# An attention cycle's roundings, rescalings and read-outs placed anew over its slots; FOX's scaling with two factors

## The reference, cut to what matters

```
p_cmp = masked_softmax(q . k_cmp * scale, blk_end <= t)          # 31 compressed keys
o_cmp = p_cmp @ v_cmp
o_slc, o_win = masked_softmax(rope(q) . rope(k) * scale, causal) @ v   # two branches
nsa   = (g0 * o_cmp + g1 * o_slc + g2 * o_win) * silu(z_a)
fox   = (masked_softmax(q . k * scale + F_q - F_k, causal) @ v) * silu(z_b)
x     = x + (sigmoid(r_a) * (nsa @ w_nsa) + sigmoid(r_b) * (fox @ w_fox)) @ w_out
```

## Time and profile before

| what | value |
| --- | --- |
| median of 3 runs | 1475.65 us |
| the profiled execution: time | 1475.33 us |
| the profiled execution: span in the profile | 1473.6 us |
| TensorE, VectorE, ScalarE, GpSimd busy | 98%, 70%, 62%, 34% of the span |
| granted TensorE clock, mean | 0.999 of full |

### The profile page before, as it was taken

How to read it: one execution, slowest core, us unless ns; L and a number is a source line. 1 busy time by engine, 2 the same in 40 slices (tenths; PEclk the granted TensorE clock), 3 DMA queues, 4 the chain that set the end, 5 groups by cost and what they waited for, 6 DMA issues and landing times.

```text
span 1473.6 us, 22913 instructions
## 1 busy us (share of the span) xinstructions
PE 1440.1 (98%) x7490; PEld 1223.7 (83%) x7490; DVE 1025.3 (70%) x2431; ACT 910.2 (62%) x1912; POOL 499.2 (34%) x578
## 2 busy tenths in 40 slices
PE   9999999999999999999999999999999999999998
PEld 7887888888888788888888888888888887888887
DVE  6847888888888874444576588888888887644444
ACT  6636888778788752223464487788778777422234
POOL 2303664565566420000021145654665564000000
PEclk9999999999999999999999999999999999999999
DMA  8232212212121233333453312212121212433332
GB/s 281 76 98 59 58 44 58 58 44 58 44 58 44 58 117 98 100 100 87 112 181 91 98 48 54 58 43 59 44 58 47 55 45 55 139 92 100 99 100 90
DMA packets 201626, 118.29 MB, mean 80 GB/s; under 512 B 9304, under 2 KB 195888, under 8 KB 201008
## 3 DMA queue, kind: packets, MB, share of 16 engines
q1 hardware_dynamic: 199120, 107.49, 26.7%
q0 software_dynamic: 1728, 8.66, 1.6%
q10 hardware_dynamic: 672, 0.83, 0.2%
HBM read 110.54 MB, written 6.42 MB: 79 GB/s over the span
## 4 chain that ended last, share of the span: by engine, by line
PE 82%; DVE 8%; ACT 5%; issue 3%; POOL 0%; DVEq 0%; ACTq 0%; POOLq 0%
PE acc L1906 52%; PE o_pair L2005 6%; PE turned L1980 6%; PE scores L1963 3%; PE scores L1965 3%; PE turned L2234 2%; ACT q_fox L909 2%; DVE prob L1465 2%; PE scores L2234 1%; DVE q_fox L1377 1%; ACT w_hi L860 1%; DVE pt_lo L1477 1%; PE turned L2158 1%; PE o_pair L2013 1%; DVE qk_raw L1333 1%
## 5 line engine op out<-in xcount | busy, mean ns | idle before, releaser
L1906 PE MATMUL acc<-u_hi,w_hi 128*128 128x512 f32 x968 | 380.4, 393 | 0.0
L1906 PE MATMUL acc<-u_lo,w_hi 128*128 128x512 f32 x968 | 378.9, 391 | 0.0
L1906 PE MATMUL acc<-u_hi,w_lo 128*128 128x512 f32 x968 | 375.8, 391 | 0.0
L1290 DVE TENSOR_TENSOR w_lo<-w_raw,w_hi 128x1024 fp32r<-128x1024 f32 x184 | 228.0, 1239 | 116.6 <-ACT w_hi L860 115.9
L860 ACT ACTIVATE w_hi<-w_raw 128x1024 fp32r<-128x1024 f32 x184 | 193.1, 1050 | 132.4 <-PE acc L1906 79.4
L981 ACT ACTIVATE prob<-prob,row_max 128x256 f32<-128x256 f32 (+3 forms) x308 | 172.7, 561 | 134.0 <-DVE row_max L1465 128.6
L1906 PEld LDWEIGHTS acc<-u_hi,w_lo 128*128 128x128 f32 x968 | 181.8, 188 | 34.8
L1906 PEld LDWEIGHTS acc<-u_hi,w_hi 128*128 128x128 f32 x968 | 181.8, 188 | 34.7 <-issue 0.2
L1906 PEld LDWEIGHTS acc<-u_lo,w_hi 128*128 128x128 f32 x968 | 181.9, 188 | 33.5 <-issue 0.2
L783 POOL TENSOR_SCALAR prob<-prob,row_inv,gates 128x384 f32<-128x384 f32 (+3 forms) x205 | 137.1, 669 | 203.2 <-DVE row_inv L1472 202.4
L1477 DVE TENSOR_TENSOR pt_lo<-turned,pt_hi 128x384 fp32r<-128x384 f32 (+3 forms) x384 | 169.6, 482 | 3.5 <-ACT pt_hi L990 3.5
(11 more groups left out here) (337 smaller groups left out, 2783.3 us busy)
## 6 DMA issues: line engine op xcount, KB each, us to landing
w_raw<-in_w_in_dram SPq DMA_DIRECT2D x140, 512.0 KB, 3.7
w_raw<-in_w_proj_nsa_dram SPq DMA_DIRECT2D x16, 512.0 KB, 3.8
w_raw<-in_w_proj_fox_dram SPq DMA_DIRECT2D x16, 512.0 KB, 3.8
w_raw<-in_w_out_dram SPq DMA_DIRECT2D x16, 512.0 KB, 3.8
x_scratch<-xT POOLq DMA_DIRECT2D x2, 2048.0 KB, 8.2
xT<-x_scratch POOLq DMA_DIRECT2D x2, 2048.0 KB, 8.7
x_nat<-in_x_dram SPq DMA_DIRECT2D x4, 512.0 KB, 6.1
c_w<-in_cmp_w_k_dram SPq DMA_DIRECT2D x4, 512.0 KB, 5.5
```

What stands on the lines that cost most here:

```text
L1290: dve.tensor_tensor(w_lo[:, par, :, 0:width], w_raw[:, par, :, 0:width], w_hi[:, par, :, 0:width], ALU.subtract).then_inc(w_lo_done, 1)
L1906: ins = pe.matmul((bank or acc[par])[0:width, :], own_w, rhs, start=(n == 0), stop=(n == 23))
```

## The change

The number of instructions of TensorE, ScalarE and VectorE stays as it is. What changes is where they stand:

- TensorE: `cmp_turn` from slot 5 to 7, `cmp_values` of head 0 from 11 to 13, and `Plan`'s costs with it: two matmuls each move from slot 7 to slot 5 and one from slot 13 to 11 (in the last cycle likewise).
- ScalarE: `cmp_copy` from slot 7 to 10; the tanh of FOX's z two slots earlier, of NSA's z one slot later.
- VectorE: `split_lo` one slot later, but for the unit whose loop index is 0; `qf_rest` one head at a time, the second two slots later; `kf_rest` of head 0 one or two slots later; FOX's z read one slot earlier; NSA's z read and silu one slot later; the read of FOX's head 1 from slot 7 to 8; `cmp_rest` from slot 8 to 12.
- GpSimd: FOX's probabilities are scaled by the reciprocal and by a column of ones, in the form of instruction that NSA's have with their gate.

```diff
-        for s, cost in ((1, 2.0), (5, 2.0), (11, 1.0), (19, 1.0)):
+        for s, cost in ((1, 2.0), (7, 2.0), (13, 1.0), (19, 1.0)):
...
-                if branch is None:
-                    ins = pool.tensor_scalar(p, p, row_inv[:, ring:ring + 1], None, ALU.mult)
-                else:
-                    gate = gates[:, qt, bass.ds(2 * pair.i + HEADS * branch + h, 1)]
-                    ins = pool.tensor_scalar(p, p, row_inv[:, ring:ring + 1], gate, ALU.mult, ALU.mult)
-                ins.then_inc(s_scaled, 1)
+                gate = ones[:, 0:1] if branch is None else gates[:, qt, bass.ds(2 * pair.i + HEADS * branch + h, 1)]
+                pool.tensor_scalar(p, p, row_inv[:, ring:ring + 1], gate, ALU.mult, ALU.mult).then_inc(s_scaled, 1)
...
-                at(plan.end[z] + 4, lambda: z_tanh_of(fox.r, 1))
+                at(plan.end[z] + 2, lambda: z_tanh_of(fox.r, 1))
                 if not cycle.first:
-                    at(max(0, Plan().end[4] + 1 - CYCLE_STEPS) + 2, lambda: z_tanh_of(nsa.r, 0))
+                    at(max(0, Plan().end[4] + 1 - CYCLE_STEPS) + 3, lambda: z_tanh_of(nsa.r, 0))
...
-                at(7, cmp_copy)
+                at(10, cmp_copy)
...
-            def qf_rest(parts):
+            def qf_rest(parts, heads):
 
                 dve.wait_ge(part_hi_done, parts + 1)
-                for h in range(2):
+                for h in heads:
                     ins = dve.tensor_tensor(q_fox[other(h), h, 0, :], qk_raw[own(h), :], q_fox[own(h), h, 0, :],
                                             ALU.subtract)
-                ins.then_inc(part_lo_done, 1)
+                if 1 in heads:
+                    ins.then_inc(part_lo_done, 1)
...
-                        at(slot + 1, lambda u=u: split_lo(*cycle.unit(u + 1)))
+                        at(slot + (2 if u else 1), lambda u=u: split_lo(*cycle.unit(u + 1)))
...
-                at(plan.end[0] + 3, lambda: qf_rest(parts))
+                at(plan.end[0] + 3, lambda: qf_rest(parts, (0,)))
+                at(plan.end[0] + 5, lambda: qf_rest(parts, (1,)))
...
-                at(key + 3, lambda: kf_rest(parts + 1, (0,), nsa.m))
+                at(key + (4 if cycle.first or cycle.last else 5), lambda: kf_rest(parts + 1, (0,), nsa.m))
...
-                at(plan.end[z] + 2, lambda: z_raw_of(*cycle.unit(z), fox.r, 1))
+                at(plan.end[z] + 1, lambda: z_raw_of(*cycle.unit(z), fox.r, 1))
...
-                    late = max(0, Plan().end[4] + 1 - CYCLE_STEPS)
+                    late = max(0, Plan().end[4] + 1 - CYCLE_STEPS) + 1
...
-                    at(7, lambda: head_output(before, 1))
+                    at(8, lambda: head_output(before, 1))
...
-                at(8, cmp_rest)
+                at(12, cmp_rest)
...
-                for slot, what in ((1, cmp_scores), (5, cmp_turn), (11, lambda: cmp_values(0)),
+                for slot, what in ((1, cmp_scores), (7, cmp_turn), (13, lambda: cmp_values(0)),
```

## The result

The changed kernel takes 1450.93 us (median of 4 runs, 1450.17 to 1451.44); the kernel before, on the same chip, 1475.42 (median of 4). The ratio is 0.9834, 95% interval 0.9817 to 0.9851. Forecast were 1450.7 and a range of 1446 to 1461. The profiled execution took 1450.78, its span is 1449.1 (before 1475.33 and 1473.6).

A forecast was written before the change was run, and what follows sets the result against it. TensorE, busy 98% of the span, bounds the kernel, so only its holes can be won: 12 x 1.45 + 2 x 1.73 + 2 x 2.0 = 24.9 us off, giving 1450.7; range 1446 to 1461.

The forecast's parts named there:

- the mechanism of slot 10: Middle cycles: a transposition waits for VectorE's pt_lo of step 4, late by queues on VectorE and ScalarE; 1.45 us each, 12 times.
- the z slots: New slots for z read-outs: free VectorE early, head 0's y_all 0.6 us sooner; nothing gained on TensorE's path in middle cycles.
- w_lo's move: VectorE's split_lo one slot later: slot 7's maximum is ready by about 228.9, so ScalarE goes on at 229.36 instead of 230.16.
- the last cycles: Last attention cycle of each layer: holes of together 3.22 us close, a new 1.3 opens; net about 2.0, bounds 0.8 and 3.2.
- The order on both engines: VectorE's and ScalarE's queues before slot 10: pt_lo ready at 234.55 and 234.95, covers of 0.6 and 0.5 before TensorE asks.
- The first cycles: First attention cycle of each layer: its whole hole of 1.73 us goes; its slot 5 wait for a maximum stays.
- the holes of 0.55, 0.84 and 1.01: Three of four TensorE holes in each layer's last cycle, the 0.55 for y_all; claimed to close by the same moves.
- kf_lo's new wait: Last cycles: key's remainder of head 0, moved from slot 14 to 15, ends after TensorE comes; new hole of 1.3 us.
- Rival B: Hole closes partly or returns two slots on, VectorE and GpSimd contending in slot 10; 1457 to 1463; 0.25 with upper C.
- Rival C: Edit misses the cause: q_fox on ScalarE starts no earlier, only pc_t's 0.77 is won; 1463; chance within B's 0.25.
- Rival D: Slower: compression chain becomes the bound, its cover falling from 5.3 to 2.5; 1490 if 5 late; chance 0.06 with its like.
- q_fox: FOX's query remainder on VectorE: second head, 0.69 us, leaves slot 8 for slot 10, shortening the queue ahead of pt_lo.

## Why the prediction was right

The total and the mechanism of slot 10 came as forecast. One step was wrong and didn't show in the total, the z slots; two were mis-sized, what w_lo's move is worth and the last cycles.

*What bounds it, and the slot 10 hole.* Right, but for a detail: the view of waits doesn't end with the three rows that the prediction calls all of them. Three more, ahead of the first attention cycle, hold 2.4 us (1.7, 0.5 and 0.2), and 2.3 of it is still there. The hole was all pt_lo, and it closed in every middle cycle: 1.51 saved in each but one, where 1.45 was said. That one, the fourth of layer 0, had been 51.86 before and gave 1.75.

*The order on both engines.* Right to 0.3 us. The prediction let VectorE end pt_lo of step 5 at 234.95, 17.17 into the cycle; it ended at 16.95. The transposition was put at 17.35 and came at 17.34.

*ScalarE.* pt_hi of step 4 was to be ready at 15.6 into the cycle; it starts at 14.97 and the pair ends at 15.84.

*The first cycles.* 1.73 said, 1.63 measured. *The last.* 2.0 said, 1.5 measured. kf_lo's new wait was said as 1.3 and is 1.39. The wrong step is "the holes of 0.55, 0.84 and 1.01 close by the same moves": that of slot 10 stays with 0.77. There w_lo stands ahead of slot 9's remainders and, begun 0.16 behind a scaling on GpSimd, takes 1.68 instead of 1.2. The prediction had weighed this contention only for slot 10 of the middle cycles.

Sum: 2 x 1.63 + 11 x 1.51 + 1.75 + 2 x 1.5 = 24.6 us, against 24.9 forecast.

*The z slots: the step that was wrong, in a sum that is right.* "None of it is on TensorE's path in middle cycles: nothing gained." Taken as an edit to the kernel before that is so (1474.83). In the change it isn't: w_lo's move needs it. With w_lo alone, and with compression and w_lo, y_all of slot 3 ends 6.37 into the cycle, behind the 6.18 at which TensorE asks. It isn't TensorE's gain that makes it late: with the compression alone TensorE gains 1.03 a cycle and y_all stays in time at 5.83, and with w_lo alone TensorE gains nothing and waits. The prediction followed w_lo to slots 7 and 11 and to its own reader, but not in slot 21, ahead of the next cycle's head; and it had y_all 0.6 sooner by the z slots and used that for the last cycles alone. The z slots bring it to 4.74. Without them 9.2 of the 24.5 us are gone. Only because the part was in the change did the total come out: that much was luck.

*w_lo: undersized.* The prediction had it as what makes ScalarE's q_fox start 0.8 earlier. The runs show a second and larger effect, 28.9 us in company against 3.2 alone: it takes w_lo out of slot 10, where q_fox's second head and GpSimd's y_all now stand. Rival B, at 0.25, named the meeting but not what keeps it away. The wait it spoke of, up to 1.3, is 0.98. The 2.00 by which the cycle is longer is more than the 0.4 to 0.8 of B, but it holds w_lo's own 1.23 too, and no run has the one without the other.

*q_fox.* The prediction counted 0.69 off VectorE's queue for it. With y_all's 0.68 put in its place this is nothing, as the 1451.52 without it shows.

*The two factors.* Sum and cost right: 0, shown by 1450.84.

*Rival C* is out: q_fox on ScalarE starts 12.19 into the cycle instead of 13.11. *Rival D* is out for the changed kernel: the compression's remainder ends at 237.76, 2.4 before its use at 240.17, where 2.5 was said. Its mechanism showed in the last cycle with the compression alone and without w_lo (1.0 and 1.3 of waiting).

Without w_lo's move the cycle is 2.00 longer: 0.35 at slot 10, 1.31 at slot 12, and 0.26 right behind that, where the third transposition of the slot waits for the next remainder. Two things stay open. The key's new slot in the middle cycles was never tried by itself. And that it is the w_lo of slot 21 which makes y_all late is read from the traces; no run moved that one alone.

## What to carry to other kernels

Parts of a schedule change don't add. Alone these four parts give -11.5, -3.2, +16.0 and -0.6 us, about +0.8 in sum; together, and with the key's new slot, they give -24.5. So an operation that is moved must be followed in every slot where it now stands, along its engine's queue to each reader, and over the cycle's end: w_lo's move pays in slot 10 and costs in slot 3 of the next cycle. And what runs on the other engine in the same place counts too: two engines with separate queues can still be one queue.

## What the runs showed of the hardware

GpSimd's one-factor scaling of 128x512 takes twice as long as the two-factor one, in one kernel, without the two factors (busy us, mean ns | idle before):
```profile
L783 POOL TENSOR_SCALAR prob<-prob,row_inv,gates 128x512 f32<-128x512 f32 x51 | 39.5, 774 | 63.1 <-DVE row_inv L1474 63.1
L780 POOL TENSOR_SCALAR prob<-prob,row_inv 128x512 f32<-128x512 f32 x25 | 39.2, 1567 | 6.9 <-DVE row_inv L1474 6.9
```
In the changed kernel FOX's 25 take 774 in the mean, as NSA's do. The 2024 of the earlier trace rows held some waiting beside it: of those 25 the median is 1571, the longest 2617. The shorter form was worth nothing in time here. The Trainium skill ("GPSIMD Engine Reference", section 3.1) would have both forms at one price; the measurement decides against it for this pair.

VectorE's operations on two SBUF inputs and GpSimd's exclude each other nearly for their whole length, and the one that has to stand back carries the wait in its own duration, not as idle time: w_lo 1.68 instead of 1.22, q_fox 1.67 instead of 0.69, y_all 2.30 instead of 1.30. Without w_lo's move y_all ends 1.14 behind w_lo and q_fox 0.56 behind y_all, each 0.13 to 0.16 less than its own length. That is the lock of the Trainium skill ("SBUF — State Buffer", "Who interferes with whom"); the trace agrees. Which of the two stands back follows the starts with a small offset: GpSimd's scaling, begun 0.16 and 0.19 earlier, kept its length and w_lo and q_fox waited; begun 0.05 or 0.08 earlier (231.85 against q_fox at 231.90, 214.94 against w_lo at 215.02, in the changed kernel), it was the one that waited. These are the starts that the profile writes down.

An operation of VectorE that has one of its two inputs in PSUM, as qk_raw has with acc, shows no such wait. In the kernel before it runs beside GpSimd's y_all (237.42 to 239.72) in its usual time:
```profile
238.49 0.68 DVE L1333 TENSOR_TENSOR qk_raw<-acc,rstd 128x512 f32<-128x512 f32 x1
```
So where an operation with both inputs in SBUF takes longer than others of its kind and shape, look at the other engine first; no view of waits lists it.
